# Narrow weights made the stationary operand: the steps of time, the router and the compressed scores of a two-block model

## What is computed

```python
# first layer, compressed branch: 8 heads in 2 groups of 4, 15 compressed keys for each group
s = jnp.einsum('bgrqd,bgkd->bgrqk', qb, kc) - slopes * (tf[:, None] - cmp_center[None, :])
p_cmp = masked_softmax(s, cmp_end[None, :] <= t[:, None])

# second layer, the last 32 columns of its input product are the steps of time
z, xbc, dt = split_cols(h @ w_in, SSM_SPLITS)
dt = jax.nn.softplus(dt.astype(jnp.float32) + dt_bias)

# mixture of 8 experts, the router
logits = (h @ router).astype(jnp.float32)
top_val, top_idx = lax.top_k(logits, TOP_K)
```

## Time and profile before

| | us |
|---|---|
| median of 3 executions | 2082.15 |
| lowest, highest | 2077.14, 2086.22 |
| the profiled execution | 2076.86 |
| its span in the trace | 2075.1 |
| TensorE busy | 1979.2 |
| VectorE busy | 1726.3 |
| ScalarE busy | 1328.1 |
| mean granted TensorE clock | 0.986 |

### The profile page before, as it was taken

One profiled execution on the slowest core, in us unless ns is written; L12 is line 12 of the kernel. 1 busy time (PEld: TensorE's weight loads), 2 busy tenths in 40 slices (PEclk: granted clock), 3 DMA queues, 4 the chain that ended last, 5 costly groups with the idle time before them and its releaser, 6 DMA issues.

```text
span 2075.1 us, 28437 instructions
## 1 busy us (share of the span) xinstructions
PE 1979.2 (95%) x10312; PEld 1642.6 (79%) x10312; DVE 1726.3 (83%) x2439; ACT 1328.1 (64%) x1977; POOL 0.2 (0%) x4
## 2 busy tenths in 40 slices
PE   6998999998989999999999999999999998999997
PEld 5777899978877788888888878878888875767785
DVE  7698878768776698989989898998989988885764
ACT  4354534355564587878888787877878875554543
POOL 0000000000000000000000000000000000000000
PEclk9999999999999999999999999999999999999999
DMA  9856689846332298989989999998999994671630
GB/s 376 292 170 220 238 308 327 281 139 209 122 106 92 74 375 328 367 331 383 371 340 369 327 358 359 358 360 334 374 326 378 372 364 156 234 252 62 223 122 21
DMA packets 154211, 560.19 MB, mean 270 GB/s; under 512 B 17232, under 2 KB 17488, under 8 KB 153936
## 3 DMA queue, kind: packets, MB, share of 16 engines
q1 hardware_dynamic: 154064, 558.29, 73.8%
HBM read 557.18 MB, written 1.05 MB: 269 GB/s over the span
## 4 chain that ended last, share of the span: by engine, by line
PE 70%; DVE 15%; ACT 6%; DMA 4%; issue 3%; DVEq 0%; SPq 0%; ACTq 0%
PE ps L526 19%; PE ps L528 19%; PE ps L527 19%; PE ps L532 10%; DVE spl L515 6%; ACT sph L503 3%; PE ps L536 3%; DVE macc L579 2%; DMA ring<-in_moe_gu 2%; DMA ring<-in_moe_down 1%; DVE arena L2167 1%; ACT arena L770 1%; DMA ring<-in_dense_gu 1%; DMA ring<-in_dense_down 0%; ACT arena L2133 0%
## 5 line engine op out<-in xcount | busy, mean ns | idle before, releaser
L503 ACT ACTIVATE sph<-ring 128x1024 fp32r<-128x1024 f32 x906 | 948.6, 1059 | 516.0 <-PE ps L528 338.3
L515 DVE TENSOR_TENSOR spl<-ring,sph 128x1024 fp32r<-128x1024 f32 x906 | 1079.0, 1219 | 239.6 <-ACT sph L503 225.5
L526 PE MATMUL ps<-sph,hH 128*128 128x512 f32 (+1 forms) x1296 | 520.5, 402 | 1.4 <-DVE hL L883 1.4
L528 PE MATMUL ps<-sph,hL 128*128 128x512 f32 (+1 forms) x1296 | 506.5, 391 | 0.0
L527 PE MATMUL ps<-spl,hH 128*128 128x512 f32 (+1 forms) x1296 | 505.4, 390 | 0.0
L528 PEld LDWEIGHTS ps<-sph,hL 128*128 128x128 f32 x1296 | 244.4, 189 | 52.3
L526 PEld LDWEIGHTS ps<-sph,hH 128*128 128x128 f32 x1296 | 245.0, 189 | 51.2 <-issue 3.9
L527 PEld LDWEIGHTS ps<-spl,hH 128*128 128x128 f32 x1296 | 245.1, 189 | 48.0 <-issue 1.0
L526 PE MATMUL ps<-sph,rH 128*128 128x512 f32 x664 | 269.2, 405 | 6.0 <-ACT arena L3121 2.3
L528 PE MATMUL ps<-sph,rL 128*128 128x512 f32 x664 | 259.9, 391 | 0.0
L527 PE MATMUL ps<-spl,rH 128*128 128x512 f32 x664 | 259.4, 391 | 0.0
(11 more groups left out here) (316 smaller groups left out, 1750.4 us busy)
## 6 DMA issues: line engine op xcount, KB each, us to landing
ring<-in_moe_gu SPq DMA_DIRECT2D x448, 512.0 KB, 5.4
ring<-in_moe_down SPq DMA_DIRECT2D x224, 512.0 KB, 5.3
ring<-in_mod SPq DMA_DIRECT2D x144, 512.0 KB, 4.7
ring<-in_w_in SPq DMA_DIRECT2D x64, 512.0 KB, 4.4
ring<-in_dense_gu SPq DMA_DIRECT2D x44, 512.0 KB, 5.3
ring<-in_ssm_w_in SPq DMA_DIRECT2D x40, 512.0 KB, 4.0
ring<-in_dense_down SPq DMA_DIRECT2D x22, 512.0 KB, 5.3
ring<-in_hyb_w_in SPq DMA_DIRECT2D x20, 512.0 KB, 6.0
```

What stands on the lines that cost most here:

```text
L503: a.activation(k.high[m % SPLITS][:, 0:w], raw[:, 0:w], ACT.Copy).then_inc(k.S.half_rounded, 1)
L515: v.tensor_tensor(k.low[m % SPLITS][:, 0:w], raw[:, 0:w], k.high[m % SPLITS][:, 0:w], ALU.subtract).then_inc(*k.tick(k.S.half_split, f"hal ...
L526: pe.matmul(out, a[0], b[0], start=start, stop=False, skip_group_check=True)
L528: return pe.matmul(out, a[1], b[0], start=False, stop=stop, skip_group_check=True)
```

## The change

In the steps of time, the narrow weight becomes the stationary operand: 128 columns of `dtw3` from column 64c on, of which the first 64 are wanted, and all 256 tokens move in one product. That makes 16 products in place of 32, whose result stands turned (features in partitions). ScalarE copies it to `dtT`, TensorE turns it back in two transposes a step later, and VectorE reads it from there. The whole chain of the steps of time moves back by one step of the generator: its first step on VectorE is now empty, and the cumulated sums stand behind piece m+2.

The router is changed in the same way, with VectorE making the copy (`lgT`). The eight products of the last norm's row are parted: four stand between the products and the turning back, four behind it. The products now wait for both token tiles of the activations' first half before they begin.

The compressed keys get 128 columns, 98 of them zero, so that each product moves 128; the scores of two tiles lie 256 columns apart, and the bias is added in two operations of 120 columns.

Around that: three memsets for the zero columns, a larger arena, and a smaller scratch for DMA descriptors that the kernel doesn't use.

```diff
@@ compressed scores
-        scores = bank[:, 120 * t:120 * t + 120].rearrange("p (g h n) -> p g h n", g=2, h=4)
         for h in range(4):
-            last = mm(pe, scores[:, :, h, :], Y.qb[:, h, t * 128:(t + 1) * 128], Y.kcT.rearrange("p (g n) -> p g n", g=2))
+            c = 256 * t + 30 * h
+            last = mm(pe, bank[:, c:c + 128], Y.qb[:, h, t * 128:(t + 1) * 128], Y.kcT)
@@ time_tensor
-    bank = banks.take(pe, "dt", "dt.in")
-    pe.wait_ge(*when("dtw.low"))
-    for t in range(NT):
-        o = bank[:, 64 * t:64 * t + 64]
-        for c in range(KD):
-            mm(pe, o, k.hH[:, c, t * 128:(t + 1) * 128], k.dtw3[:, c, :], c == 0, False)
-            last = mm(pe, o[:, 0:32], k.hL[:, c, t * 128:(t + 1) * 128], k.dtw3[:, c, 0:32], False, c == 7)
-    last.then_inc(*tick(S.dt_tensor, "dt.mm"))
+    bank = banks.take(pe, "dt.T", "dt.moved")
+    pe.wait_ge(*when("dtw.low"))
+    w = k.dtw3.rearrange("p a n -> p (a n)")
+    for c in range(KD):
+        mm(pe, bank[:, 0:T], w[:, 64 * c:64 * c + 128], k.hH[:, c, :], c == 0, False)
+        last = mm(pe, bank[:, 0:T], w[:, 64 * c:64 * c + 128], k.hL[:, c, :], False, c == 7)
+    last.then_inc(*tick(S.dt_tensor, "dt.mm"))
+    yield
+    bank = banks.take(pe, "dt", "dt.in")
+    pe.wait_ge(*when("dt.moved"))
+    for t in range(NT):
+        last = turn(pe, k, bank[:, 128 * t:128 * t + 128], M.dtT[:, t * 128:(t + 1) * 128])
+    last.then_inc(*tick(S.dt_tensor, "dt.back"))
     yield
     yield
     bank = banks.take(pe, "cum", "dt.toend")
@@ time_scalar
+    a.wait_ge(*when("dt.mm"))
+    a.activation(M.dtT, k.banks[k.bank_of.get("dt.T", 0)][:, 0:T], ACT.Copy).then_inc(*tick(S.dt_scalar, "dt.moved"))
+    yield
     a.wait_ge(*when("dt.abs"))
@@ time_vector
+    yield
-    v.wait_ge(*when("dt.mm"))
+    v.wait_ge(*when("dt.back"))
@@ router_tensor
+    bank = k.banks_turn.take(pe, "route.T", "route.moved")
+    pe.wait_ge(*when("row3.low"))
+    w = k.row3.rearrange("p a n -> p (a n)")
+    for c in range(KD):
+        for t in range(NT):
+            if c % 4 == 0:
+                pe.wait_ge(*when(f"n3.low{t}.{c // 4}"))
+        mm(pe, bank[:, 0:T], w[:, 16 * c:16 * c + 128], k.hH[:, c, :], c == 0, False)
+        last = mm(pe, bank[:, 0:T], w[:, 16 * c:16 * c + 128], k.hL[:, c, :], False, c == 7)
+    last.then_inc(*tick(S.route_tensor, "route.products"))
+    row_tensor(pe, k, "fnorm", k.V["fnorm"], 8, (), 0, 4)
     bank = k.banks_turn.take(pe, "route", "route.lg")
+    pe.wait_ge(*when("route.moved"))
+    for t in range(NT):
+        last = turn(pe, k, bank[:, 128 * t:128 * t + 128], E.lgT[:, t * 128:(t + 1) * 128])
     last.then_inc(*tick(S.route_tensor, "route.logits"))
+    row_tensor(pe, k, "fnorm", k.V["fnorm"], 8, (), 4, 8)
     bank = k.banks_turn.take(pe, "place", "route.place")
-    row_tensor(pe, k, "fnorm", k.V["fnorm"], 8, ())
     pe.wait_ge(*when("route.sel"))
@@ router_vector
+    v.wait_ge(*when("route.products"))
+    v.tensor_copy(E.lgT, k.banks[k.bank_of.get("route.T", 0)][:, 0:T]).then_inc(*tick(S.route_vector, "route.moved"))
```

More of the change, by code:

```diff
@@ L32 @@
 NI = EXPERT_TILES // 2
-ARENA = 16008
+ARENA = 17000
 INV_2PI = 1.0 / (2.0 * math.pi)
@@ L291, in __init__ @@
         self.hid, self.htm = A.get(4, 30), A.get(4, 30)
-        self.kcT = A.get(30)
+        self.kcT = A.get(128)
         self.fac = A.get(NT, 8)
@@ L333, in __init__ @@
         self.diag = A.get(NT, 128)
+        self.dtT = A.get(T)
         self.ss, self.rr, self.t8 = A.get(8), A.get(8), A.get(8)
@@ L362, in __init__ @@
         self.turned = A.get(256)
+        self.lgT = A.get(T)
         self.dispT = [k.dtw3[:, 4 * i:4 * i + 4, :].rearrange("p (t a) n -> p t (a n)", t=2) for i in range(2)]
@@ L890, in square, with row_tensor @@
                  accum_out=k.st[:, 56 + 2 * t + c:57 + 2 * t + c]).then_inc(*k.tick(k.S.squared, f"{name}.squared{2 * t + c}"))
-def row_tensor(pe, k, name, cols, n, waits):
+def row_tensor(pe, k, name, cols, n, waits, first=0, stop=None):
     for event in waits:
         pe.wait_ge(*k.when(event))
-    for c in range(0, n, 4):
+    for c in range(first, n if stop is None else stop, 4):
         bank = k.banks_turn.take(pe, f"{name}.{c}", f"{name}.copied{c}")
@@ L1111, in hybrid_scalar @@
         advance(live)
-    a.activation(k.dtw3[:, :, 0:32], k.dtw[:, :, :], ACT.Copy).then_inc(*k.tick(k.S.small_split, "dtw.high"))
-    a.activation(k.row3[:, :, 0:8], k.router, ACT.Copy).then_inc(*k.tick(k.S.small_split, "row3.high"))
+    a.activation(k.dtw3[:, 0:8, 0:32], k.dtw[:, :, :], ACT.Copy).then_inc(*k.tick(k.S.small_split, "dtw.high"))
+    a.activation(k.row3[:, 0:8, 0:8], k.router, ACT.Copy).then_inc(*k.tick(k.S.small_split, "row3.high"))
     split_scalar(a, k, k.stream.first["hyb_out"] + 3 + SPLITS)
@@ L1143, in hybrid_vector @@
     Y = k.Y
+    v.memset(Y.kcT[:, 30:128], 0.0).then_inc(*k.tick(k.S.vector_step, "keys.zero"))
     for g in range(2):
@@ L1170, in hybrid_vector @@
     v.wait_ge(*k.when("dtw.high"))
-    v.tensor_tensor(k.dtw3[:, :, 32:64], k.dtw[:, :, :], k.dtw3[:, :, 0:32], ALU.subtract).then_inc(*k.tick(k.S.vector_step, "dtw.low"))
+    v.memset(k.dtw3[:, 8, :].bitcast(F32), 0.0).then_inc(*k.tick(k.S.vector_step, "dtw.low"))
+    v.memset(k.row3[:, 8:15, :].bitcast(F32), 0.0).then_inc(*k.tick(k.S.vector_step, "dtw.low"))
+    v.tensor_tensor(k.dtw3[:, 0:8, 32:64], k.dtw[:, :, :], k.dtw3[:, 0:8, 0:32], ALU.subtract).then_inc(*k.tick(k.S.vector_step, "dtw.low"))
     v.wait_ge(*k.when("row3.high"))
-    v.tensor_tensor(k.row3[:, :, 8:16], k.router, k.row3[:, :, 0:8], ALU.subtract).then_inc(*k.tick(k.S.vector_step, "row3.low"))
+    v.tensor_tensor(k.row3[:, 0:8, 8:16], k.router, k.row3[:, 0:8, 0:8], ALU.subtract).then_inc(*k.tick(k.S.vector_step, "row3.low"))
     for c in range(4):
@@ L1572, in compressed_vector @@
     v.wait_ge(*when("cmp.scored"))
-    v.tensor_tensor(pf, k.banks[k.bank_of.get("cmp.s", 0)][:, 0:240], k.C["cmpb"], ALU.add).then_inc(*tick(S.cmp_vector, "cmp.biased"))
+    for t in range(NT):
+        scores = k.banks[k.bank_of.get("cmp.s", 0)][:, 256 * t:256 * t + 120].rearrange("p (h g n) -> p g h n", h=4, g=2)
+        v.tensor_tensor(Y.pc[:, t, :].rearrange("p (g h n) -> p g h n", g=2, h=4), scores,
+                        k.C["cmpb"][:, 120 * t:120 * t + 120].rearrange("p (g h n) -> p g h n", g=2, h=4), ALU.add).then_inc(*tick(S.cmp_vector, "cmp.biased"))
     v.wait_ge(*when("cmp.biased"))
@@ L2059, in time_vector @@
     S, tick, when, M = k.S, k.tick, k.when, k.M
-    bv = k.banks[k.bank_of.get("dt", 0)][:, 0:128].rearrange("p (t n) -> p t n", t=2)
-    v.wait_ge(*when("dt.mm"))
+    yield
+    bv = k.banks[k.bank_of.get("dt", 0)][:, 0:256].rearrange("p (t n) -> p t n", t=2)
+    v.wait_ge(*when("dt.back"))
     v.tensor_tensor(M.sp, bv[:, :, 0:32], k.rows32[:, 0, :].unsqueeze(1).broadcast_to([128, NT, 32]), ALU.add).then_inc(*tick(S.dt_vector, "dt.bias"))
@@ L2493, in router_tensor @@
     S, tick, when, E = k.S, k.tick, k.when, k.E
+    bank = k.banks_turn.take(pe, "route.T", "route.moved")
[9 more added lines that the diff above has]
+    row_tensor(pe, k, "fnorm", k.V["fnorm"], 8, (), 0, 4)
     bank = k.banks_turn.take(pe, "route", "route.lg")
-    pe.wait_ge(*when("row3.low"))
+    pe.wait_ge(*when("route.moved"))
     for t in range(NT):
[L2497 to L2503, removed]
+        last = turn(pe, k, bank[:, 128 * t:128 * t + 128], E.lgT[:, t * 128:(t + 1) * 128])
     last.then_inc(*tick(S.route_tensor, "route.logits"))
+    row_tensor(pe, k, "fnorm", k.V["fnorm"], 8, (), 4, 8)
     bank = k.banks_turn.take(pe, "place", "route.place")
-    row_tensor(pe, k, "fnorm", k.V["fnorm"], 8, ())
     pe.wait_ge(*when("route.sel"))
@@ L2525, in router_vector @@
     S, tick, when, E = k.S, k.tick, k.when, k.E
-    bv = k.banks[k.bank_of.get("route", 0)][:, 0:32].rearrange("p (t n) -> p t n", t=2)
+    v.wait_ge(*when("route.products"))
+    v.tensor_copy(E.lgT, k.banks[k.bank_of.get("route.T", 0)][:, 0:T]).then_inc(*tick(S.route_vector, "route.moved"))
+    bv = k.banks[k.bank_of.get("route", 0)][:, 0:256].rearrange("p (t n) -> p t n", t=2)
     wk = E.wk
```

6 lines of the change are left out of this document (3 added, 3 removed).

## The result

| | before | after |
|---|---|---|
| median, us | 2078.99 (5 executions) | 2095.62 (5 executions) |
| lowest to highest | 2076.28 to 2086.22 | 2092.85 to 2105.31 |
| ratio, 95% interval | | 1.0086 (1.0062 to 1.0110) |
| profiled execution, its span | 2076.86, 2075.1 | 2092.85, 2091.1 |

The change made the kernel slower by 0.9%, some 17 us. The time after lies outside the predicted range, and on the side that I gave 0.03.

The account below looks back on a forecast made before the run. TensorE, busy for 95% of the span and carrying 70% of the chain, was taken as the bound. Gains of 1.2 + 0.8 + 0.7 = 2.7 us from the median 2082.15 gave 2079.4 us, range 2072.5 to 2086.

Parts of the forecast that it names:

- the side that I gave 0.03: Whole kernel: slower by more than the 0.5% (10.4 us) that a measurement can tell from no change; chance 0.03.
- the rest is nothing: Memsets at the begin and the layer's end and the smaller scratch: no effect on the time.
- a difference that grows in the experts: Sign that the forecast is wrong: time changing in the experts, which it held to be unchanged.
- Part A: Compressed scores: clock stays up behind products of 128 columns; gain 1.2 us, bounds -0.2 and 1.7.
- Part B: Steps of time: 16 products for 32, then a 3.2 us wait for `dt.a`; gain 0.8 us, bounds -0.9 and 2.1.
- Part C: Router: places start 1.9 us earlier, gather may cost up to 1.7 more; gain 0.7 us, bounds 0.2 and 1.9.
- (1): All three places: the clock holds everywhere, gain 5.7 us, 2076.5 us; chance 0.2.
- (2): Sums, m+3 and gather: clock falls at the wait for `dt.a` and stays low, slower, 2083.0 us; chance 0.2.
- (3): All three places: products get shorter but no stage's end does, 2082.2 us; chance 0.13.
- (4): New products: weight load not hidden, 16 products at 0.23 us at each place, 2081.5 us; chance 0.01.

## Why the prediction was wrong, and where it was right

**The step that failed** is "the rest is nothing", and with it the sentence that held the experts to be unchanged. I priced what the lines of the diff do, and took two of them, the new sizes of `dtw3` and `row3`, for bookkeeping. They are the 17 us. I had named the sign of it, "a difference that grows in the experts", but given the case no chance and no price, so the range couldn't hold it. None of the rivals was this one. With like remainders the new arithmetic gave ratios of 0.9994, 0.9985, 0.9995 and 0.9986; the forecast, 2079.4 of 2082.15, is 0.9987.

Those four agree with the forecast, and no interval of them excludes a ratio of 1.0000; the old arithmetic with the small scratch stands at 0.9983. So the total doesn't prove the sum. The parts can be read from the traces. The chain of after at the scores and at the steps of time:

```profile
123.46 2.46 PE ps L534 x18
...
126.36 0.84 PE ps L534 x8
...
439.70 3.03 PE ps L534 x24
```

The granted clock in stretches of 1 us (the columns of the earlier trace rows):

```profile
127.00:128.00 1.00, 1.00 (x6) 0.84 (x6) 0.93 (x5) 0.00 (x0) 0.00 (x0) 1.00 0.75 172
440.00:441.00 1.00, 1.00 (x11) 1.00 (x10) 1.00 (x2) 0.00 (x0) 0.00 (x0) 1.00 0.00 0
446.00:447.00 1.00, 1.00 (x12) 1.00 (x11) 0.95 (x2) 0.98 (x2) 0.00 (x0) 1.00 0.48 82
...
459.00:460.00 1.00, 1.00 (x7) 1.00 (x6) 0.23 (x1) 0.00 (x0) 0.00 (x0) 0.50 0.90 348
...
709.00:710.00 1.00, 1.00 (x6) 1.00 (x6) 0.91 (x5) 0.00 (x0) 0.00 (x0) 0.50 0.00 0
```

And instructions in order of time:

```profile
439.90 0.28 PE L534 MATMUL ps<-hL,dtw 128*128 128x256 f32 x1
440.02 0.28 PE L534 MATMUL ps<-hH,dtw 128*128 128x256 f32 x1
...
455.50 0.83 PE L534 MATMUL ps<-arena,cst 128*128 128x32 f32 x6 [3.16 <-DVE arena L2090]
...
460.79 0.38 ACT L2147 ACTIVATE arena<-ps 128x256 f32<-128x256 f32 x1 [6.14 <-PE ps L530]
...
700.16 2.35 DVE L517 TENSOR_TENSOR spl<-ring,sph 128x1024 fp32r<-128x1024 f32 x2
...
705.81 0.88 PE L534 MATMUL ps<-arena,cst 128*128 128x8 f32 x6 [1.51 <-DVE arena L2570]
707.75 6.43 PE L534 MATMUL ps<-arena 128*128 128x128 f32 x32 [1.07 <-DVE arena L2623]
...
714.03 0.38 PE L538 MATMUL ps<-cst,arena 128*128 128x128 f32 x2
```

**Part A** had its mechanism right, and its size if anything too small. The clock stays at 1.00 behind the scores, the eight records take 0.84 for 1.58 us, and the group of 18 takes the same 2.46. From piece 20 to piece 40 the four profiled executions with the old arithmetic take 128.0, 129.1, 129.7 and 130.0 us, the ten with the new one 125.5 to 128.1, with a mean of 126.8: 2.4 us less, for the forecast 1.2 and its upper bound 1.7. The granted clock accounts for a part of it. Behind the scores it is low for 3.4 us in the kernel before and in the one with the small scratch, for 6.8 us (125 to 132) in the kernel before with the repairs, and never in the ten. In the fourth old one, at the places of after, it is low for 6.8 us too, but from 117 on, ahead of the scores at 124.4: that is not the scores' doing. The two with the shorter stretch, 128.0 and 129.7, lie 2.1 us above the mean of the ten. The last 0.4 us stay open.

**Part B** came out of the queues as laid out, but its gain did not. Sixteen products 0.12 apart; they and the gate row take 3.03 us (1.92 + 0.96 forecast), with the clock at 1.00 at 440 and 446, where it was 0.83 and 0.50. TensorE waits for `dt.a` for 3.16 us (3.2 forecast). Then the clock falls, as I took it to, inside m+3. ScalarE's first copy of the convolution comes 460.79 - 439.70 = 21.09 us behind the first product, where it came 460.72 - 438.82 = 21.90 behind it: 0.81 us, forecast 0.8. That the number fits is luck: each side is one execution, and the traces of the other kernels, with the same arithmetic, differ among themselves by more. The chain and the clock with the old arithmetic and the small scratch, then the sums and the clock behind them with the new arithmetic and both remainders 0:

```profile
444.11 3.73 PE ps L532 x32
...
446.00:447.00 1.00, 1.00 (x11) 1.00 (x11) 0.00 (x0) 0.00 (x0) 0.00 (x0) 1.00 0.00 0
```
```profile
453.89 0.83 PE L536 MATMUL ps<-arena,cst 128*128 128x32 f32 x6 [3.06 <-DVE arena L2092]
...
456.00:457.00 1.00, 1.00 (x10) 1.00 (x10) 0.97 (x4) 0.00 (x0) 0.00 (x0) 1.00 0.86 135
```

In the first all 32 narrow products run at full clock, 3.73 us for 5.31, and so they do in the old arithmetic at the places of after; the clock falls some microseconds later. The first copy then comes 20.33 and 20.22 us behind the first product, and 21.01 in the kernel before with the repairs. In the second the clock holds behind 3.06 us of waiting, m+3 takes 2.96 us, and the copy comes after 19.64; in the other eight with the new arithmetic and without the repairs the clock falls, m+3 takes 4.21 to 5.01, and the copy comes after 20.90 to 22.30. The means are 20.8 us (three kernels with the old arithmetic, without repairs) and 21.0 (nine with the new). So no gain at B is shown. The stretch says the same: from piece 100 to piece 140 the old arithmetic takes 175.3 to 177.0 us and the new one 175.7 to 179.4. The prediction took the fall of the clock inside the old products, read from one trace, for a fixed part of their price.

**Part C** had its mechanism right and one term too small. From VectorE's first low part behind the norm (702.51 before, 700.16 after) the places start 5.65 us later for 7.62 (710.13 before), 1.97 us earlier, forecast 1.9. But the gather of 32 records then runs at half clock: 6.43 us for 3.84, 2.6 more, where I had said "up to 1.7". Its two transposes behind it come 13.87 us after that low part, for 13.20 before (715.71). So C is a loss of 0.7 us here, and not a gain of 0.7; with 5.47 us for the gather, as in the kernel with the pad, it is a gain of 0.4. Here too one execution says little: from that low part to the transposes the nine kernels with the new arithmetic take 12.82 to 14.12 us and the four with the old one 13.19 to 15.86, with the gather at 5.47 to 6.76 us in all nine, at 5.54 in one of the four and at 3.84 in the others.

**The rivals.** (1) The clock holds everywhere: no, 0.50 at 459 and at 709 in after; behind the sums it held in one of nine. (2) It stays low behind both waits: it did in after, but m+3 cost less than this rival's price (4.39 us for 2.96, 1.4 more and not 2.4) and the gather more. (3) No stage's end is shortened: nothing is shown at B, and A is shortened. (4) The weight load isn't hidden: no, the new products start 0.12 us apart with a full load each, at 439.90 and 440.02. The prediction set 0.23 us for this case. The rule of the Trainium skill that it named ("TensorE: Matmul & The Clock Gate", Part 3, "The mechanism") lets a weight load overlap a matmul in flight only where the row groups differ, though the same section also speaks of loads that go ahead into a background weight buffer. The trace disagrees with the first.

## A version that beats both

At B and C the products of TensorE had become shorter, and behind each stood a wait with a low clock after it. So I put something else there: the cumulated sums go one step later on all three engines, and one 512-column constant is multiplied in each of the two waits of the router. The pad of 64 bytes is in it too.

```diff
+        self.pads = sb("pads", [128, 16])
         self.high = [sb(f"sph{i}", [128, QUARTER], F32R) for i in range(SPLITS)]
 def time_tensor(pe, k, banks):
...
-    yield
-    yield
+    yield from idle(3)
     bank = banks.take(pe, "cum", "dt.toend")
 def time_scalar(a, k):
...
-    yield from idle(3)
+    yield from idle(4)
     a.wait_ge(*when("dt.toend"))
 def time_vector(v, k):
...
     yield
+    yield
     bank = k.banks[k.bank_of.get("cum", 0)]
 def router_tensor(pe, k):
...
+    fill(pe, k, k.banks_turn, 1)
     pe.wait_ge(*when("route.sel"))
...
     mm(pe, bank[:, 8:16], k.C["ones"], E.sel[:, 0, :], False, True).then_inc(*tick(S.route_tensor, "route.before"))
+    fill(pe, k, k.banks_turn, 1)
```

> The new arithmetic with a pad of 64 bytes ahead of sph0, so that weight parts and activation parts again start at like remainders, and two repairs. Steps of time: the cumulated sums are taken one step of the item list later on TensorE, VectorE and ScalarE, so that TensorE no longer stands idle for about 3 us ahead of them. Router: TensorE multiplies one 512-column constant ahead of its wait for the choice and one behind the places, in the 1.5 us and 1.1 us in which it stood idle, so that the gather of the first expert (32 records in 5.5 us with that pad) should find the clock up (3.8 us). My theory: about 3 us less in the steps of time and 1 to 1.7 us less in the router than the same kernel without them, 2074 to 2077 us in all. Rival: the state-space stage is paced by the splits on ScalarE and VectorE, what TensorE saves at the sums it waits for elsewhere in the stage, and the time stays at 2078 to 2080.

Measured: 2069.68 us (2066.32 to 2071.32, six executions), ratio 0.9948 (0.9932 to 0.9965), 10.9 us under the median of before beside it and 25.9 us under that of after. It is below the 2074 that I expected at best. Its trace at the sums and the gather, in order of time, and the clock behind them:

```profile
454.14 0.83 PE L535 MATMUL ps<-arena,cst 128*128 128x32 f32 x6 [0.18 <-DVE arena L2090]
...
695.16 2.35 DVE L518 TENSOR_TENSOR spl<-ring,sph 128x1024 fp32r<-128x1024 f32 x2
...
699.14 1.02 PE L535 MATMUL ps<-cst 128*128 128x512 f32 x2
...
700.72 0.83 PE L535 MATMUL ps<-arena,cst 128*128 128x8 f32 x6 [0.56 <-DVE arena L2573]
701.41 1.10 PE L535 MATMUL ps<-cst 128*128 128x512 f32 x2
...
702.63 3.84 PE L535 MATMUL ps<-arena 128*128 128x128 f32 x32
...
706.30 0.38 PE L539 MATMUL ps<-cst,arena 128*128 128x128 f32 x2
```
```profile
457.00:458.00 1.00, 1.00 (x11) 1.00 (x10) 0.52 (x1) 0.97 (x2) 0.00 (x0) 1.00 0.81 274
...
703.00:704.00 1.00, 1.00 (x12) 1.00 (x11) 0.93 (x6) 0.00 (x0) 0.00 (x0) 1.00 0.00 0
```

The wait for `dt.a` is 0.18 us for 3.16, the gather is back at 3.84 us with the clock at 1.00, and the router's stretch from low part to transposes takes 11.14 us for 13.87. From piece 100 to 140 it takes 173.0 us, under every other kernel (175.3 to 179.4); from 140 to 160, 113.0 (114.8 to 121.3 in the others). The second is 4.5 us less than in the kernel that has only the pad (117.5). The router explains 12.83 - 11.14 = 1.7 of them; the rest stays open.

Was it the new arithmetic, or would the repairs have helped the old one as well? The same edits, without the pad, in the kernel before:

> The kernel before, with its own arithmetic and places, and the two repairs of the run with later sums and filled waits (the sums one step later on the three engines, one 512-column constant multiplied ahead of the wait for the choice and one behind the places). Theory: the new arithmetic gave TensorE its 2 us in each place and lost them again in two waits that the old one did not have (3.1 us ahead of the cumulated sums where the old work waited 0.7 us; a gather of 32 records in 5.5 us where the old one took 3.8 us). Then the repairs have little to repair in the old work: at most 0.7 us at the sums, nothing at the gather, 2078 to 2081 us and a ratio of 0.9985 to 1.001. Rival: the repairs shorten the state-space stage by another way (the splits of the stage and the scans come to stand differently), whatever the arithmetic: 2072 to 2075 us, a ratio of 0.996 to 0.998.

Measured: 2081.11 us, ratio 0.9999 (0.9986 to 1.0013). In the order of time its sums wait for nothing, as theory said, and its router only moves the places back, from 7.62 us behind the low part to 8.58:

```profile
461.95 0.75 PE L532 MATMUL ps<-arena,cst 128*128 128x32 f32 x6
...
708.24 2.35 DVE L515 TENSOR_TENSOR spl<-ring,sph 128x1024 fp32r<-128x1024 f32 x2
...
716.82 0.73 PE L532 MATMUL ps<-arena,cst 128*128 128x8 f32 x6
...
718.62 3.84 PE L532 MATMUL ps<-arena 128*128 128x128 f32 x32
```

The rival, by which the repairs act alone, is out. The turned operands are worth about 0.5% of this kernel, but only together with the repairs of the waits behind them, and with the operands' remainders kept alike. No run has one repair without the other, so which of them gives how much is not shown.

## What to carry to other kernels

A tensor that grows moves all that are laid out behind it. Compare where the operands of the costliest instructions start before and after a change, and don't call a new size nothing; if code that nobody touched gets slower evenly at an unchanged clock, count the distances of the starts and look at the addresses. And where an edit takes time from an engine that then waits for another, the gain is only there once the wait has been filled or moved, since the low clock behind it may cost as much as was saved. Where the clock falls differed here from trace to trace with the same arithmetic, so read a stage from several traces before you price it.

## What the runs showed of the hardware

- The price of a product depends on where its two operands start in SBUF, the on-chip memory, against each other, by their remainders modulo 128 bytes (or 256, which no run here tells apart): like (64 and 64, 0 and 0) 227 ns for 512 columns and 120 for 256; unlike (0, 32 or 96 against 64, 64 against 0) 232 to 236 and 117 to 118. The absolute place doesn't count: 15,360 bytes lower changed nothing.
- In after the clock fell behind 3.16 us of waiting and six products of 32 columns, and the gather found it at 0.50 behind two waits of 1.51 and 1.07 us with six products of 8 columns between them. With 512-column products in the latter two, TensorE found it at 1.00. Behind the sums it fell in eight of nine kernels with such a wait (3.06 to 3.21 us) and held at 1.00 in one (3.06 us).
- Whether the clock falls inside the 32 narrow products at the steps of time differed between the traces of the old arithmetic: it did in before and in before with the repairs (5.14 and 5.38 us from the first start to that of the product behind them), and not with the small scratch or at the places of after (3.56 us both).
- A product of the split parts (one record each) with a stationary operand of 128 columns and a moving one of 256 costs 0.12 us at full clock, load included; with 64 or 32 columns moving it cost 0.11 (16 of them from 438.82 to 440.60 in before).
